# Splitting the latent query and value operands of a two-block transformer kernel

## The reference

```python
qh = q.reshape(bsz, s, DSA_HEADS, DSA_HEAD_DIM)
q_lat = jnp.einsum('bshd,hld->bshl', qh, w_uk)
...
    logits = jnp.einsum('bqhl,bqkl->bqhk', qlb, c_sel).astype(jnp.float32) * (DSA_HEAD_DIM ** -0.5)
    p = jax.nn.softmax(logits, axis=-1).astype(c.dtype)
    o_lat = jnp.einsum('bqhk,bqkl->bqhl', p, c_sel)
    o = jnp.einsum('bqhl,hld->bqhd', o_lat, w_uv)
```

## Time and profile before

| | |
|---|---|
| median of 3 runs | 1278.51 us (1278.12 to 1279.11) |
| the profiled execution | 1278.12 us |
| its span, first to last instruction | 1276.0 us |
| TensorE busy / idle in the span | 1267.5 us / 8.5 us |
| VectorE busy, ScalarE busy | 762.3 us, 594.4 us |
| 32-bit matmuls at lines 2455 and 2495 | 4 and 4, two records each |

### The profile page before, as it was taken

How to read it: one execution, slowest core, us unless ns; L and a number is a source line. 1 busy time by engine, 2 the same in 40 slices (tenths; PEclk the granted TensorE clock), 3 DMA queues, 4 the chain that set the end, 5 groups by cost and what they waited for, 6 DMA issues and landing times.

```text
span 1276.0 us, 16938 instructions
## 1 busy us (share of the span) xinstructions
PE 1267.5 (99%) x6329; PEld 1058.7 (83%) x6329; DVE 762.3 (60%) x1555; ACT 594.4 (47%) x1240; POOL 40.3 (3%) x79
## 2 busy tenths in 40 slices
PE   9999999999999999999999999999999999999998
PEld 7888777898888888888888888888878788999987
DVE  5367775754555446447574677775545534976664
ACT  5367665543453345335553334663335543463633
POOL 1000000100000000001100000000000000000000
PEclk9999999999999999999999999999999999999999
DMA  7243442126552646232523232112221025758431
GB/s 249 100 146 111 132 124 84 67 99 188 137 147 90 202 128 198 82 117 99 194 71 116 99 132 99 34 67 99 99 99 67 33 99 173 190 153 228 132 133 66
DMA packets 28481, 155.84 MB, mean 122 GB/s; under 512 B 3560, under 2 KB 3820, under 8 KB 12400
## 3 DMA queue, kind: packets, MB, share of 16 engines
q1 hardware_dynamic: 23208, 132.80, 29.7%
q0 software_dynamic: 2304, 16.78, 6.9%
q10 hardware_dynamic: 2888, 5.18, 1.3%
HBM read 146.35 MB, written 4.20 MB: 118 GB/s over the span
## 4 chain that ended last, share of the span: by engine, by line
PE 96%; DVE 1%; issue 1%; DMA 0%; ACT 0%; POOL 0%; SPq 0%; ACTq 0%; POOLq 0%; DVEq 0%
PE bank L2071 26%; PE bank L2073 26%; PE bank L2072 26%; PE sc L2242 3%; PE tp L2251 2%; PE ob L2308 1%; PE ob L2266 1%; PE sc L2073 1%; PE sc L2072 1%; PE sc L2071 1%; PE bank L2176 1%; PE bank L2186 1%; PE bank L2193 1%; DMA w_raw<-in_weights 0%; PE ob L2073 0%
## 5 line engine op out<-in xcount | busy, mean ns | idle before, releaser
L2071 PE MATMUL bank<-xT_hi,w_hi 128*128 128x512 f32 (+1 forms) x1040 | 407.0, 391 | 0.1
L2073 PE MATMUL bank<-xT_hi,w_lo 128*128 128x512 f32 (+1 forms) x1040 | 395.6, 380 | 0.0
L2072 PE MATMUL bank<-xT_lo,w_hi 128*128 128x512 f32 (+1 forms) x1040 | 395.1, 380 | 0.0
L1283 DVE TENSOR_TENSOR w_lo<-w_raw,w_hi 128x512 fp32r<-128x512 f32 x404 | 257.5, 686 | 140.2 <-ACT w_hi L730 138.6
L730 ACT ACTIVATE w_hi<-w_raw 128x512 fp32r<-128x512 f32 x404 | 226.7, 621 | 78.0 <-PE bank L2073 67.7
L2071 PEld LDWEIGHTS bank<-xT_hi,w_hi 128*128 128x128 f32 x1040 | 195.8, 188 | 39.4 <-issue 4.5
L2073 PEld LDWEIGHTS bank<-xT_hi,w_lo 128*128 128x128 f32 x1040 | 195.6, 188 | 37.9
L2072 PEld LDWEIGHTS bank<-xT_lo,w_hi 128*128 128x128 f32 x1040 | 196.1, 189 | 34.9 <-issue 1.2
L738 ACT ACTIVATE arena<-bank 128x512 f32<-128x512 f32 x74 | 43.8, 597 | 137.8 <-PE bank L2073 132.6
L2071 PE MATMUL bank<-w_hi,act_hi 128*128 128x512 f32 (+1 forms) x264 | 102.7, 389 | 0.0
L2073 PE MATMUL bank<-w_hi,act_lo 128*128 128x512 f32 (+1 forms) x264 | 101.2, 383 | 0.0
(11 more groups left out here) (284 smaller groups left out, 1773.9 us busy)
## 6 DMA issues: line engine op xcount, KB each, us to landing
w_raw<-in_weights SPq DMA_DIRECT2D x99, 1024.0 KB, 4.9
arena<-in_weights POOLq DMA_DIRECT2D x16, 1024.0 KB, 9.2
arena<-in_weights SPq DMA_DIRECT2D x9, 1024.0 KB, 8.3
arena<-in_bias ACTq DMA_DIRECT2D x16, 256.0 KB, 2.9
act_lo<-act_lo SPq DMA_DIRECT2D x24, 128.0 KB, 2.6
x_sb<-in_x SPq DMA_DIRECT2D x4, 512.0 KB, 6.6
w_raw<-in_weights SPq DMA_DIRECT2D x4, 512.0 KB, 8.1
x_dram<-x_sb SPq DMA_DIRECT2D x1, 2048.0 KB, 12.3
```

Source lines behind the costliest of these rows:

```text
L1283: nc.vector.tensor_tensor(w_lo[SPLIT_AT[b]][:, cols], w_raw[SLOT[b]][:, cols], w_hi[SPLIT_AT[b]][:, cols].bitcast(F32), ALU.subtract).then ...
L2071: nc.tensor.matmul(ps, hi_l, hi_r, start=first, stop=False, skip_group_check=onto)
L2072: nc.tensor.matmul(ps, hi_l, lo_r, start=False, stop=False, skip_group_check=onto)
L2073: return nc.tensor.matmul(ps, lo_l, hi_r, start=False, stop=last, skip_group_check=onto)
```

## The change

Both groups of 32-bit matmuls become `product` calls on split operands. ACT rounds and DVE subtracts the two small weight tiles (`wuk_hi`, `wuk_lo`, `wuv_hi`, `wuv_lo`) once, after the fox attention. The four query banks are now rounded by ACT into `bq_hi`, and DVE makes `bq_lo` from the same bank; the bank is freed by DVE's instruction. Each head's `ob` is rounded by ACT into `olat_hi`, DVE makes `olat_lo`, and PE waits for that. The new tiles lie over memory that is free by then: `rows_r` is the token rows `x_sb` with the two gain rows, seen as the reduced type.

```diff
+        with nc.sbuf_tensor("rows_r", [P, TT * D + 2 * D], F32R) as rows_r:
+            pass
...
-        bq = view(4096, KW, S)
+        bq_hi, bq_lo = (rows_r[:, at:at + KW * S].rearrange("p (a s) -> p a s", s=S) for at in (0, KW * S))
...
-        olat = view(4096 + 2 * S, S)
+        wuk_hi, wuk_lo = (arena_r[:, at:at + S].rearrange("p (a b) -> p a b", b=P) for at in (2048, 2048 + S))
+        wuv_hi, wuv_lo = (rows_r[:, TT * D + D + at:TT * D + D + at + S].rearrange("p (a b) -> p a b", b=P) for at in (0, S))
+        olat_hi, olat_lo = arena_r[:, 4096 + 2 * S:4096 + 3 * S], arena_r[:, 4096 + 3 * S:4096 + 4 * S]
...
 (ACT)
+            act.wait_ge(latent_loaded, 32)
+            act.wait_ge(pv_done, U_DSA)
+            nc.scalar.activation(wuk_hi, wukT, ACT.Copy).then_inc(latent_rounded, 1)
+            act.wait_ge(latent_split, 1)
+            nc.scalar.activation(wuv_hi, wuv, ACT.Copy).then_inc(latent_rounded, 1)
             for i in range(2):
                 for c in range(2):
-                    read_out(bq[:, 2 * i + c, :], USE["b_q"] + 2 * i + c)
+                    e = USE["b_q"] + 2 * i + c
+                    act.wait_ge(bank_full, e + 1)
+                    nc.scalar.activation(bq_hi[:, 2 * i + c, :], bank[e % 4][:, :], ACT.Copy).then_inc(bq_rounded, 1)
                 split(FIRST["b_q"] + i + 2)
...
-                    nc.scalar.activation(olat, ob[:, :], ACT.Copy).then_inc(olat_ready, 1)
+                    nc.scalar.activation(olat_hi, ob[:, :], ACT.Copy).then_inc(olat_rounded, 1)
...
 (DVE)
+            dve.wait_ge(latent_rounded, 1)
+            nc.vector.tensor_tensor(wuk_lo, wukT, wuk_hi.bitcast(F32), ALU.subtract).then_inc(latent_split, 1)
+            dve.wait_ge(latent_rounded, 2)
+            nc.vector.tensor_tensor(wuv_lo, wuv, wuv_hi.bitcast(F32), ALU.subtract).then_inc(latent_split, 1)
+
+            def split_bq(i):
+                for h in range(2 * i, 2 * i + 2):
+                    e = USE["b_q"] + h
+                    dve.wait_ge(bq_rounded, h + 1)
+                    nc.vector.tensor_tensor(bq_lo[:, h, :], bank[e % 4][:, :], bq_hi[:, h, :].bitcast(F32), ALU.subtract).then_inc(bank_free[e % 4], 1)
+
             for b in range(FIRST["b_q"], FIRST["gate_a0"]):
                 step(rounds, 2)
                 split(b + 2)
+                if b in (FIRST["b_q"] + 1, FIRST["b_q"] + 2):
+                    split_bq(b - FIRST["b_q"] - 1)
...
+                    dve.wait_ge(olat_rounded, h + 1)
+                    nc.vector.tensor_tensor(olat_lo, ob[:, :], olat_hi.bitcast(F32), ALU.subtract).then_inc(olat_split, 1)
                     dve.wait_ge(ydsa_ready, h + 1)
...
 (PE)
-                pe.wait_ge(latent_loaded, 32)
+                pe.wait_ge(latent_split, 1)
...
-                    nc.tensor.matmul(sc[n % 2][:, :], wukT[:, h, :], bq[:, h, :], start=True, stop=True).then_inc(prep_ready, 1)
+                    product(sc[n % 2][:, :], wuk_hi[:, h, :], wuk_lo[:, h, :], bq_hi[:, h, :], bq_lo[:, h, :], True, True).then_inc(prep_ready, 1)
...
-                pe.wait_ge(olat_ready, g + 1)
-                nc.tensor.matmul(ob[:, :], wuv[:, g, :], olat, start=True, stop=True).then_inc(ydsa_ready, 1)
+                pe.wait_ge(latent_split, 2)
+                pe.wait_ge(olat_split, g + 1)
+                product(ob[:, :], wuv_hi[:, g, :], wuv_lo[:, g, :], olat_hi, olat_lo, True, True).then_inc(ydsa_ready, 1)
```

More of the change, by code:

```diff
@@ L426, in build @@
         o_free, o_rounded = sem("o_free"), sem("o_rounded")
-        olat_ready, ydsa_ready = sem("olat_ready"), sem("ydsa_ready")
+        olat_rounded, olat_split, ydsa_ready = sem("olat_rounded"), sem("olat_split"), sem("ydsa_ready")
+        latent_rounded, latent_split, bq_rounded = sem("latent_rounded"), sem("latent_split"), sem("bq_rounded")
         act_rounded, act_split = sem("act_rounded"), sem("act_split")
```

## The result

The changed kernel takes 1290.14 us (median of 6 runs, 1289.73 to 1291.28) against 1278.43 us for the kernel before (6 runs): a ratio of 1.0093, with a 95% interval of 1.0082 to 1.0104. It is slower, by 11.7 us. The time lies 3.1 us above the forecast and within 0.3 us of the rival in which the clock falls in the gaps.

What follows compares the result with a forecast made beforehand. PE, busy 1267.5 of 1276.0 us, was taken as the bound. 1278.12 - 1.46 (products) + 9.54 (gaps) + 0.44 (head 1) = 1286.64, forecast as 1287.0 us; own range 1285.5 to 1288, 8 in 10 range 1284.5 to 1292.5.

Steps and rivals of the forecast that it cites:

- the rival in which the clock falls in the gaps: PE's clock drops to half in both query-bank gaps, adding 3.4 us: 1290.4 us, chance 0.35.
- PE has no slack: PE never waits mid-program, so each microsecond taken from its stream is won and each wait put in is lost.
- The products, -1.46 us: Eight 32-bit matmuls become three reduced ones each: latent queries save 0.76 us, the way back 0.70.
- The small weight tiles, 0: ACT's rounding and DVE's subtraction before the selection's rounds hide in idle time; at most 2.6 us without that cover.
- The gaps, 2 x 4.77 us: PE waits twice for DVE's subtraction to free a query bank, queued behind a weight block's four subtractions: 9.54 us added.
- the lower bound: PE's restart after DVE frees a bank takes near 0.03 us, not the 0.25 taken; the gap is then 4.55 us.
- Head 1, +0.44 us: On the way back, head 1's late copy makes PE wait for DVE's subtraction: 0.44 us, between 0 and 0.8.
- the case without it: The forecast itself: two idle gaps at the query banks without a fall of the clock, 1287.0 us, chance 0.49.
- The argument for it: The trace's only fall came 4.1 us after PE's last matmul started, so a gap of 5.0 us can be long enough.
- the one against it: The 4.1 us delay comes from one fall only and may be longer at another moment.
- the clock's price: From the warm-up's 16 matmuls in 3.41 us: 1.3 to 1.7 us per slow stretch, 3.4 for two falls.
- The rule on idle gaps: The skill says PE gaps of more than about 3 us return the clock to half; by it the clock rival results.

Runs made afterwards that it cites:

- e5: The changed kernel with 18 small 32-bit matmuls, results unused, put in PE's order ahead of each of the two waits: 1286.20 us.
- e1: The changed kernel with DVE's subtractions that free the query banks moved ahead of the weight block's four subtractions: 1276.63 us against 1278.22 for the kernel before.
- e4: The kernel before, all matmuls in 32 bits, with query banks freed late by a DVE subtraction behind the weight block: 1292.73 us against 1278.22.
- e3: The changed kernel with only the way back split; latent queries and their banks' release by ACT as in the kernel before: 1277.90 us against 1278.22.
- e2: The changed kernel with only the latent queries split; the way back as in the kernel before: 1291.46 us against 1278.22.
- e6: The changed kernel with the query banks' two subtractions behind the first of the weight block's four parts instead of the fourth: 1285.75 us.
- e8: The changed kernel with the banks' subtractions ahead of the weight block, but behind a wait for ACT's first rounding of that block: 1283.59 us.
- e9: The changed kernel with the banks' subtractions ahead of the weight block, but behind a wait for ACT's reading of the last full bank: 1280.40 us.

## Why the prediction was right, and where it was not

The time of 1290.14 us lies in the range of 8 in 10, 1284.5 to 1292.5, since that range took in the clock's case; it lies outside the forecast's own range of 1285.5 to 1288.

**PE has no slack.** Held. Each gap comes back in full in the time: in e5 two gaps of 4.57 and 0.11 make 9.4 us, and the kernel is 9.6 above e1.

**The products, -1.46 us.** Held as far as it can be measured: three matmuls step through in 0.68 us at head 0, and e1 is 1.6 us faster than the kernel before, 1.2 of it in the span. The rule of the Trainium skill on four passes (FP8 and Floating Point Precision, TensorE Precision Notes) would have made it 1.8; the runs can't tell the two apart.

**The small weight tiles, 0.** Held: ACT and DVE finish them at 907.1 us, and e1, which has them, has no wait there.

**The gaps, 2 x 4.77 us.** The mechanism was right, and e1 and e4 show it from both sides; the size was 4.56 and 0.11 for the first matmul after it, 4.67. The restart is near the lower bound: 0.06 us from DVE's end to the first matmul's start.

**Head 1, +0.44 us.** Measured 0.39, and the other heads don't wait. e3, 0.3 us faster where 0.70 less 0.39 was due, agrees in size but can't be told from no change.

**Which case.** Here the forecast chose wrong. The step that failed is the choice of the likeliest case: the clock's fall had 0.35 and the case without it 0.49. The argument for it and the one against it both set the gap beside the delay of one fall, 4.1 us after the last matmul's start. The runs show two things in place of that. The delay is not fixed: it is 3.0 us (923.04 - 920.07) and 4.2 us in the changed kernel and 4.8 us in e2; it did come out longer once, as the argument against had it, and the clock fell all the same. And a gap need not outlast the delay: the gaps of 2.76 us in e6, well below 4.1, make the clock fall after PE has resumed.

That the rival's 1290.4 came out within 0.3 us is in part luck. The products, head 1 and the time around them made 1277.5 us by the sum, and e1 measured 1276.6, 0.9 less; the gaps were 0.2 too long (9.54, 9.34 measured); the two falls were 0.8 too cheap (3.4, 4.2 measured). For the profiled execution the clock's price is (4.98 + 6.18) us of low-clock work times the share lost, 1 - 0.2275/0.4275 = 0.47 (ten steps from 925.45 to 929.72 make 0.4275 each), which is 5.2 us; with the gaps 14.6, where 1291.28 less e1's profiled 1276.70 is 14.58. Over all runs it is 4.2 us. The price came from 16 matmuls at the program's start, 3.41 us, which was too short a model: each slow stretch lasted 6.8 us here. Nor does a row show that those 16 ran at the lower level: the granted clock reads 1.00 from 0 to 4 us, and their steps are 1.6 times those of the next 14, not twice.

**The rule on idle gaps.** The Trainium skill (TensorE: Matmul & The Clock Gate, Why this matters for your kernels) warns of gaps of more than about 3 us. It named the right rival. With its figure the runs don't agree: 2.6 us of idle PE made the clock fall in e6, and 2.0 us did once in two in e8.

## What to carry to other kernels

When an edit gives a buffer's release to another engine, walk that engine's order from the release backwards: what stands ahead of it may be waiting for the very engine that waits for the buffer. Put such a release ahead of any work that depends on the waiting engine's latest result; here one moved call turned 11.7 us lost into 1.6 us gained. Where PE is the bound, price an idle gap of 2 us or more with a slow stretch behind it, and if the gap can't be removed, fill it with matmuls whose results nobody reads.

## What was not expected of the hardware

The granted clock fell after idle stretches as short as 2.60 us, and in one of two cases after 1.99 us, but not after 1.47 us (the ten runs of e9 lie within 0.6 us). It can fall after PE has resumed: at 923.64, where matmuls had started again at 923.17. Once low it stayed low for 6.8 us both times in the changed kernel, although PE was busy for 5 to 6 us of them, and for 3.4 us in e6 (the mean of 0.74 from 926 to 928 puts its return at 927.04). The length of the gap alone doesn't set it: in e2 the first stretch lasted 3.4 us and the second 6.8, behind equal gaps of 4.57 us. What exactly decides the moment and the length was not tried.
